# One block of a 31-tap depthwise convolution moved from TensorE to VectorE in a three-block transformer kernel

## What is computed

```
proj = x @ w_in[l]                      # 1024 -> 3072: q, f_raw, i_val, g_out, conv_val, conv_gate, 512 each
f = lb + (1.0 - lb) * sigmoid(f_raw);  k = 1.0 - f;  log_f = log(f)
o = hgrn2_chunkwise(heads(q), heads(k), heads(i_val), heads(log_f))     # 4 heads of 128
u = conv_val * sigmoid(conv_gate)
c = conv_general_dilated(u, conv_w[l], padding=[(30, 0)], feature_group_count=512) + conv_b[l]
o_b = silu(layer_norm(c, conv_ln_g[l], conv_ln_b[l]))
x = layer_norm(ALPHA * x + concatenate([o_a, o_b]) @ w_out[l])
```

## Time and profile before

| | us |
|---|---|
| median of three runs | 4168.96 |
| the profiled execution's own time | 4166.99 |
| its span (first to last instruction) | 4165.2 |
| TensorE busy | 3723.9 (89%) |
| VectorE busy | 2556.6 (61%) |
| ScalarE busy | 1189.2 (29%) |
| GpSimd busy | 345.6 (8%) |

### The profile page before, as it was taken

How to read it: one execution, slowest core, us unless ns; L and a number is a source line. 1 busy time by engine, 2 the same in 40 slices (tenths; PEclk the granted TensorE clock), 3 DMA queues, 4 the chain that set the end, 5 groups by cost and what they waited for, 6 DMA issues and landing times. The chain is left out here.

```text
span 4165.2 us, 50974 instructions
## 1 busy us (share of the span) xinstructions
PE 3723.9 (89%) x19025; PEld 3216.6 (77%) x19025; DVE 2556.6 (61%) x4155; ACT 1189.2 (29%) x2077; POOL 345.6 (8%) x281
## 2 busy tenths in 40 slices
PE   8998988899977897999999989999988889688998
PEld 7876755687845796799999979999867768566876
DVE  4544676554755465388999867777644437655434
ACT  1101132210031332133678833333321123402300
POOL 0000010000000020003212322222100000000000
PEclk9999999999989798999999999999999989789999
DMA  4322201222732001158888999999612111022232
GB/s 151 97 74 81 87 5 41 104 91 83 258 115 81 0 1 56 58 179 289 308 295 306 324 320 333 330 336 327 230 61 86 63 38 46 1 81 80 82 109 72
DMA packets 198968, 591.00 MB, mean 142 GB/s; under 512 B 22128, under 2 KB 80368, under 8 KB 196720
## 3 DMA queue, kind: packets, MB, share of 16 engines
q1 hardware_dynamic: 161920, 454.34, 32.7%
q0 software_dynamic: 36864, 134.23, 9.0%
HBM read 536.07 MB, written 52.43 MB: 141 GB/s over the span
## 5 line engine op out<-in xcount | busy, mean ns | idle before, releaser
L484 DVE CAST w_hi<-w_ring 128x1024 fp32r<-128x1024 f32 (+1 forms) x336 | 238.4, 709 | 491.9 <-PE banks L438 449.7
L71 DVE TENSOR_TENSOR w_lo<-w_ring,w_hi 128x1024 fp32r<-128x1024 f32 (+1 forms) x336 | 424.6, 1264 | 11.5
L2631 PE MATMUL out_ps<-w_hi,v_hi 128*128 128x384 f32 x1024 | 345.8, 338 | 41.2 <-DVE w_lo L71 41.1
L438 PE MATMUL banks<-x_hi,w_hi 128*128 128x512 f32 x896 | 356.2, 398 | 28.0 <-DVE x_lo L71 28.0
L2331 PE MATMUL up_ps<-h_hi,u_hi 128*128 128x384 f32 x1024 | 351.3, 343 | 20.0 <-DVE u_lo L71 19.9
L438 PE MATMUL banks<-x_lo,w_hi 128*128 128x512 f32 x896 | 354.9, 396 | 0.0
L438 PE MATMUL banks<-x_hi,w_lo 128*128 128x512 f32 x896 | 354.7, 396 | 0.0
L2631 PE MATMUL out_ps<-w_lo,v_hi 128*128 128x384 f32 x1024 | 344.4, 336 | 0.0
L2631 PE MATMUL out_ps<-w_hi,v_lo 128*128 128x384 f32 x1024 | 344.2, 336 | 0.0
L2331 PE MATMUL up_ps<-h_lo,u_hi 128*128 128x384 f32 x1024 | 343.7, 336 | 0.0
L2331 PE MATMUL up_ps<-h_hi,u_lo 128*128 128x384 f32 x1024 | 343.7, 336 | 0.0
(11 more groups left out here) (546 smaller groups left out, 7722.8 us busy)
## 6 DMA issues: line engine op xcount, KB each, us to landing
expert_tiles<-peer_u SPq DMA_DIRECT2D x128, 512.0 KB
expert_tiles<-peer_v SPq DMA_DIRECT2D x128, 512.0 KB
w_ring<-w_in SPq DMA_DIRECT2D x104, 512.0 KB, 3.6
w_ring<-ffn_up SPq DMA_DIRECT2D x88, 512.0 KB, 3.6
w_ring<-w_ff SPq DMA_DIRECT2D x64, 512.0 KB, 3.7
ada_ring<-w_ada SPq DMA_DIRECT2D x48, 512.0 KB, 5.7
peer_acts<-act_ring SPq DMA_DIRECT2D x128, 192.0 KB
peer_gates<-staging SPq DMA_DIRECT2D x12, 2048.0 KB
```

Source lines behind the costliest of these rows:

```text
L71: return nc.vector.tensor_tensor(self.lo[at], value, self.hi[at].bitcast(F32), ALU.subtract)
L438: last = nc.tensor.matmul(banks[:, j, s, 0:n], a[:, u % 2, k, :], b[:, g * kg + k, x_from + c:x_from + c + n], start=(g == 0 and k == 0 an ...
L484: nc.vector.tensor_copy(w_parts.hi[:, u % 2], ring[:, u % slots]).then_inc(hi_ready, 1)
L2631: last = nc.tensor.matmul(out_ps[:, b, P:T], a[:, n % 2, b * P:b * P + P], r[:, n % 2, :], start=(n == 0 and part == 0), stop=(n == NKEYS ...
```

## The change

Convolution block 1 is computed by VectorE beside the in-projection, with blocks 2 and 3, so that 93 taps (6 in twelve of the turns, 7 in three) run there, with a wait for the tap three back instead of two. Block 0 stays where it was, and the groups of diagonals and matmuls inside the decay levels, the eviction of block 1 and its PSUM bank go.

```diff
-        own_taps = [(cb_, j) for j in range(TAPS) for cb_ in (2, 3)]
+        own_taps = [(cb_, j) for j in range(TAPS) for cb_ in (1, 2, 3)]
...
-                    dve.wait_ge(own_tap, n - 1)
+                    dve.wait_ge(own_tap, n - 2)
...
-        conv_ps = p.ps(conv_banks, "conv_ps", [P, 2, T])
+        conv_ps = p.ps(conv_banks, "conv_ps", [P, 1, T])
...
-        taps = [(cb_, j) for cb_ in range(2) for j in range(TAPS)]
+        taps = [(0, j) for j in range(TAPS)]
...
-            def group(s):
-
-                return TAPS + TAPS * s // (LEVELS + 1), TAPS + TAPS * (s + 1) // (LEVELS + 1)
-
...
                         nc.scalar.activation(decay[:, l % 2, :], decay[:, l % 2, :], ACT.Exp).then_inc(decay_ready, 1)
-                    diagonals(act, *group(l))
                     if l == 0:
                         act.wait_ge(diag_used, TAPS)
                         nc.scalar.activation(mix[:, 4, :], conv_ps[:, 0, :], ACT.Identity, bias=conv_b[:, 0:1]).then_inc(conv_out, 1)
-                act.wait_ge(diag_used, 2 * TAPS)
-                nc.scalar.activation(mix[:, 5, :], conv_ps[:, 1, :], ACT.Identity, bias=conv_b[:, 1:2]).then_inc(conv_out, 1)
-                act.wait_ge(conv_out, 2)
+                act.wait_ge(conv_out, 1)
...
                         last.then_inc(scored, 1)
-                    convolve(pe, *group(s))
```

## The result

The changed kernel takes 4185.88 us in the median of nine runs, the kernel before 4172.32 in nine runs. The medians are 13.6 us apart; the ratio worked out from all the runs is 1.0037 with a 95% interval of 1.0024 to 1.0049, that is +15.4 us (10 to 20). The prediction said 4174 with a range up to 4183.

The account below looks back on a forecast made before the run. The prediction took TensorE to bound the in-projection and VectorE, stretched by GpSimd's product, the levels. In-projection +6.9, levels -3.6 and clock +2.0 gave +5.3 us, from 4168.96 to 4174 us, range 4163 to 4183.

Parts of the forecast that it names:

- no room above 5 taps: In-projection: turns of 6 taps cost VectorE 5.92 us, of 7 6.58, against TensorE's 5.60; +6.9 us in all.
- The exclusion of GpSimd and VectorE's two-input operations: Decay levels: GpSimd's product and VectorE operations with two SBUF inputs do not run together; first distance 3.22 us, otherwise 1.23.
- the free takes: Decay levels: VectorE's four takes (2.43 us) read PSUM and were taken to run beside GpSimd's product.
- the level of 7.90 us at the full clock: Decay levels without taps: one level takes 7.90 us against 8.02, GpSimd's product now delaying the product of q.
- the levels' -3.6 us at the full clock: Removing the levels' taps: 4.7 us gained, 1.1 lost to later scores; between -12.3 and 0.
- part 3: Clock in the decay levels: TensorE's idle gaps of 4.1 us make some sets slow; +2.0 us taken.
- the upper bound of 13.2: Most the lower clock could cost in the levels: 4 x 1.46 + 2 x 3.7 us.
- the exposed sets: Sets 6 and 7 of the scores, which nothing covers; 3.7 us each at 1.2 GHz, a third of the chance counted.
- rival A: Decay levels: clock falls before every set from 2 to 7; +16.5 us in all, 4185; chance 0.10.
- B: Decay levels: GpSimd's product falls wholly under the takes, levels of 6.1 us; -5.4 us in all, 4163.6; chance 0.10.
- C: In-projection: each hand-over costs 0.3 us, +10.1 there; +8.5 us in all, 4177.5; chance 0.12.
- D: In-projection: with three chains a tap comes at 0.6 us and turns fit; no difference, 4168.7; chance 0.06.

Follow-up runs that it names:

- the filled kernel: Changed kernel plus four matmuls by the identity, result unread, behind each of the first six sets of scores; ratio to the kernel before 1.0006.
- The third buffer: Changed kernel with three buffers instead of two for the products kd, GpSimd and VectorE waiting for the set before the last; ratio to the kernel before 1.0003.
- GpSimd's wait: Changed kernel, GpSimd's product held until the next level's distances are made; ratio to before 1.0000. Same wait in the kernel before: 0.999.
- the spread taps: Changed kernel with GpSimd's product delayed to the next distances and 93 taps laid into VectorE's pauses, 19 in the scan stage; ratio to before 1.0002.

## Why the prediction was wrong

**Right.** The in-projection: no room above 5 taps, 5.92 us a turn forecast and 5.93 in the mean measured, +6.9 forecast and +6.8 measured. The Trainium skill's rule in "Vector Engine (DVE) Microarchitecture Reference", section "Points that are easy to get wrong" (half throughput for such an operation), is contradicted again: a tap stayed at 0.66 us. The exclusion of GpSimd and VectorE's two-input operations, the free takes, and the level of 7.90 us at the full clock (7.91 measured) are right too. So is the levels' -3.6 us at the full clock, nearly: the filled kernel has -2.4 with one set still slow.

**The step that failed** is part 3, "I take 2.0 us". The clock cost 9.9 us against the filled kernel (12.7 in the second profile of the changed one), near the upper bound of 13.2. Nor does the 2.0 follow from the terms that it names: set 2 at 1.46 and a third of the 7.4 of the exposed sets are 3.9. Two things in the mechanism were wrong besides.

First, which sets would be slow. The prediction read the idle time in front of a burst (2.99 us harmless, 4.24 not) and took "a burst behind a late start leaves a shorter gap for the next" as a protection. It was none. Here are the changed kernel's sets on TensorE's timeline:

```profile
620.00 5.26 PE L1016 MATMUL score_ps<-kd 128*128 128x128 f32 x32 [5.06 <-DVE kd L988]
628.86 5.47 PE L1016 MATMUL score_ps<-kd 128*128 128x128 f32 x32 [3.61 <-DVE kd L988]
...
658.20 6.58 PE L1016 MATMUL score_ps<-kd 128*128 128x128 f32 x32 [3.63 <-DVE kd L988]
666.70 5.47 PE L1016 MATMUL score_ps<-kd 128*128 128x128 f32 x32 [1.92 <-DVE kd L988]
```

All seven sets with decay were slow, also behind gaps of 3.6 and 1.92 us. The Trainium skill's rule, named in rival A ("TensorE: Matmul & The Clock Gate", section "HAM oscillation"), says that bursts separated by waits keep starting at the low clock. This trace agrees for the gaps of 3.6 us, more than the row of 2.99 us did; the case on the page has waits of about 3 to 5 us, so it does not speak of the sets behind 1.92.

Second, what a slow set costs. The working let GpSimd start 2.01 us behind the distances whatever the clock. But GpSimd also waits for the set in front (two buffers). At the full clock that wait ends before ScalarE's exponential does (in the filled kernel the set from 636.26 is over at 640.10, and the exponential, not shown, at 640.62). At 1.2 GHz it ends last, and GpSimd then stands in front of the product of q with its whole length, so a level takes 8.9 to 10.2 us (10.2 to 10.3 throughout in the second profile), where rival A's working had 7.90 + 1.46 = 9.4. The third buffer took 6.6 us of it away.

**Rival A** was right in its cause, and its number, 4185 forecast, 4185.88 and 4185.14 measured, is in part luck. Its two errors (not every set was slow throughout; the wait was left out) cancel, and the kernel before, which it put at 4168.96, has medians of 4172.32 and 4175.10 beside those runs: its +16.5 us stands against 13.6 and 10.0 between the medians, or 15.4 and 13.8 by the ratios. Its chance of 0.10 was too low. Rivals B, C and D fell: the exponential alone did not bring GpSimd under the takes, the hand-overs cost next to nothing, and VectorE was the bound.

## What to carry to other kernels

Work on TensorE that looks free may be what holds its clock: before taking matmuls out of a loop of short bursts, price the loop with every burst at 1.2 GHz and follow each wait on a burst through at that length, since one that never mattered can end last. Where a product on GpSimd and VectorE's operations on two SBUF inputs take turns, put GpSimd's beside VectorE's reads of PSUM, by a wait if need be: in the kernel before that was worth 5.5 us of the levels, more than the 2.4 that taking all 31 taps out of them gave with the clock held up by fillers. And count room per turn, not per stage: four taps left 1.0 us, which holds one more and not two.

## What was not expected of the hardware

Sets of 128-column matmuls were slow behind gaps as short as 1.92 us (e.g. the last set above, 5.47 us). With GpSimd's wait, four of the six sets behind gaps of 1.92 to 2.23 us were slow, while in the kernel before a gap of 2.99 us in front of small matmuls did nothing. The same gap of 1.92 us stands in front of a set of 3.84 us at 631.96 and of one of 5.47 at 651.17. In that run and the one with the spread taps, every set that came behind a set at the full clock was slow, and of the seven behind a slow set five were at the full clock. With two filler matmuls of 512 columns behind each of the first six sets (gaps of 0.5 us) the sets were at 2.4 GHz but for the first, behind a gap of 3.27 us; with the spread taps also the last was slow, behind 1.92 us and with no filler in front. So the gap in front does not decide alone. The same program also differs from execution to execution in this: 0.76 and 0.70 in the levels, 2.8 us apart.
